# High and low words of the split weights interleaved in one SBUF tile, on a two-block forward pass

## What is computed

```
first_block:  h = x + y @ w_out          y = [conv group, pool group] of rmsnorm(x) @ w_in + b_in
              h = h + swiglu(rmsnorm(h)) w_gate, w_up: 1024 x 2816, w_down: 2816 x 1024
              return rmsnorm(h)
second_block, layer 0:  gated ("fox") attention, 16 heads of 64; layer norm; conv FFN; layer norm; shared k1, k2, v
              layer 1:  differential attention, 8 heads; layer norm; conv FFN; layer norm
conv FFN:     u = x @ w_in (1024 x 5632); causal conv of width 3 over tokens; silu(g) * val; @ w_out (2816 x 1024)
```

## Time and profile before

| | us |
|---|---|
| three runs, median | 1811.86 |
| three runs, lowest and highest | 1810.9, 1812.83 |
| the profiled execution, its own time | 1808.84 |
| span from its first to its last instruction | 1807.0 |
| TensorE busy | 1762.7 |
| weight loads busy, beside the matmuls | 1476.5 |
| VectorE, ScalarE, GpSimd busy | 765.9, 796.0, 1032.3 |

### The profile page before, as it was taken

How to read it: one execution, slowest core, us unless ns; L and a number is a source line. 1 busy time by engine, 2 the same in 40 slices (tenths; PEclk the granted TensorE clock), 3 DMA queues, 4 the chain that set the end, 5 groups by cost and what they waited for, 6 DMA issues and landing times.

```text
span 1807.0 us, 26859 instructions
## 1 busy us (share of the span) xinstructions
PE 1762.7 (98%) x8755; PEld 1476.5 (82%) x8755; DVE 765.9 (42%) x1382; ACT 796.0 (44%) x1674; POOL 1032.3 (57%) x926
## 2 busy tenths in 40 slices
PE   8999999999999999999999999999999999999997
PEld 6879888888887888788888888877777888888887
DVE  7973000001235556553333322487875533333224
ACT  5644332322245555464444422555565644444231
POOL 6966555555562333466666665655554666666651
PEclk9999999999999999999999999999999999999999
DMA  4312333333334454223333233333332233332332
GB/s 153 94 47 82 105 93 93 93 88 109 94 89 115 126 134 120 85 75 100 103 94 93 82 110 88 82 93 78 86 82 71 72 110 97 93 101 82 105 91 98
DMA packets 327252, 171.94 MB, mean 95 GB/s; under 512 B 43458, under 2 KB 316948, under 8 KB 327188
## 3 DMA queue, kind: packets, MB, share of 16 engines
q1 hardware_dynamic: 327172, 171.12, 33.7%
q10 hardware_dynamic: 16, 0.00, 0.0%
HBM read 152.15 MB, written 2.10 MB: 85 GB/s over the span
## 4 chain that ended last, share of the span: by engine, by line
PE 86%; DVE 9%; ACT 2%; issue 1%; POOL 1%; DMA 0%; DVEq 0%; SPq 0%; ACTq 0%
PE bank L983 24%; PE bank L985 23%; PE bank L984 23%; DVE score L2266 3%; PE attended L983 2%; PE attended L984 2%; PE attended L985 2%; PE turned L1424 1%; PE attended L1440 1%; PE bank L1056 1%; PE bank L1068 1%; DVE xres L2165 1%; PE bank L1069 0%; PE score L1417 0%; PE score L1407 0%
## 5 line engine op out<-in xcount | busy, mean ns | idle before, releaser
L742 POOL TENSOR_TENSOR WL<-raw,WH 128x512 fp32r<-128x512 f32 (+3 forms) x656 | 777.6, 1207 | 539.8 <-ACT WH L1605 537.2
L983 PE MATMUL bank<-XL,WH 128*128 128x512 f32 x1432 | 568.5, 397 | 3.7 <-DVE work L2577 1.2
L985 PE MATMUL bank<-XH,WL 128*128 128x512 f32 x1432 | 557.9, 390 | 0.0
L984 PE MATMUL bank<-XH,WH 128*128 128x512 f32 x1432 | 557.3, 389 | 0.0
L1605 ACT ACTIVATE WH<-raw 128x512 fp32r<-128x512 f32 (+3 forms) x656 | 338.4, 566 | 293.2 <-PE bank L985 186.5
L985 PEld LDWEIGHTS bank<-XH,WL 128*128 128x128 f32 x1432 | 269.4, 188 | 56.9
L983 PEld LDWEIGHTS bank<-XL,WH 128*128 128x128 f32 x1432 | 269.7, 188 | 55.9 <-DVE work L2577 1.5
L984 PEld LDWEIGHTS bank<-XH,WH 128*128 128x128 f32 x1432 | 269.9, 188 | 50.3
L983 PE MATMUL bank<-HL,WH 128*128 128x512 f32 (+1 forms) x528 | 198.6, 376 | 0.0
L985 PE MATMUL bank<-HH,WL 128*128 128x512 f32 (+1 forms) x528 | 198.4, 376 | 0.0
L984 PE MATMUL bank<-HH,WH 128*128 128x512 f32 (+1 forms) x528 | 198.4, 376 | 0.0
(11 more groups left out here) (366 smaller groups left out, 2524.9 us busy)
## 6 DMA issues: line engine op xcount, KB each, us to landing
raw<-in_ffn_w_in SPq DMA_DIRECT2D x88, 512.0 KB, 3.7
raw<-in_w_gate SPq DMA_DIRECT2D x22, 512.0 KB, 3.6
raw<-in_w_up SPq DMA_DIRECT2D x22, 512.0 KB, 3.7
raw<-in_ffn_w_out SPq DMA_DIRECT2D x28, 384.0 KB, 3.2
raw<-in_ffn_w_out SPq DMA_DIRECT2D x28, 320.0 KB, 3.2
raw<-in_a_w_in SPq DMA_DIRECT2D x16, 512.0 KB, 3.9
raw<-in_kv_w SPq DMA_DIRECT2D x32, 256.0 KB, 3.0
raw<-in_w_in SPq DMA_DIRECT2D x12, 512.0 KB, 3.7
```

The costliest lines, as they stand in the source:

```text
L742: pool.tensor_tensor(wl, x, wh, ALU.subtract).then_inc(w_lo, 1)
L983: pe.matmul(out_, wh, xl, start=start, stop=False)
L984: pe.matmul(out_, wh, xh, start=False, stop=False)
L985: return pe.matmul(out_, wl, xh, start=False, stop=stop)
```

## The change

WH and WL were two tiles, each of 4 slots of 8 x 128 words in a partition. They become views of one tile with a last dimension of 2: high words at even, low words at odd places. All code that uses WH and WL stays as it is, so each access to them, by ScalarE (write), GpSimd (read and write) and TensorE (weight load), now has a step of two words, 8 bytes, where it had one of 4. The space in a partition is the same, 32 KB.

```
-        WH = sb("WH", [P, SLOTS, DT, P], F32R)
-        WL = sb("WL", [P, SLOTS, DT, P], F32R)
+        weights = sb("weights", [P, SLOTS, DT, P, 2], F32R)
+        WH, WL = weights[:, :, :, :, 0], weights[:, :, :, :, 1]
```

## The result

The changed kernel takes 1852.34 us (median of four runs, 1851.71 to 1857.44) against 1811.38 us for the kernel before in the same comparison: ratio 1.0233, 95% interval 1.0219 to 1.0247. It is slower by 41 us. The forecast was 1811.9 us, with a range to 1819 us. The profiled execution has a span of 1851.0 us, 44.0 us longer than before.

The account below looks back on a forecast made before the run. TensorE was taken as the bound, busy 1762.7 of 1807.0 us. Zero each for TensorE, ScalarE and GpSimd, added to the median of 1811.86 us, gave 1811.9 us, with a range from 1808.5 to 1819 us.

Parts of the forecast that it names:

- What bounds the kernel: Whole kernel: TensorE is the bound, busy 1762.7 of 1807.0 us, and hardly ever waits for weights, 1.3 us.
- ScalarE and GpSimd at zero: Stepped write of WH, read of WH and write of WL: claimed to add 0 us each to the kernel.
- high ends: Upper bounds for the stepped accesses of ScalarE and GpSimd: twice the time of now, 1242 ns for ScalarE's write.
- I take zero: TensorE's stepped weight loads: claimed to cost nothing, from L2242's 6 ns in 256 words and the moving stream's pace.
- It could take twice as long and just stay hidden: Under 512-column matmuls a weight load has 0.226 us and needs 0.113, so twice its time was claimed to cost nothing.
- the range's upper end: 1819 us: the small producer slowdown, and 0.006 us more on each 256-column matmul, 7 us.
- The last sign that I gave: In the changed profile: 512-column starts moving from 0.226 us would mean a weight load of over twice its time.
- the forecast's own rule: 512-column matmuls: they keep 0.226 us until loads need more than that, and pay beyond it.
- The 0.006 us margin at 256 columns: Under 256-column matmuls a load has 0.119 us and needs 0.113, so nearly all of any slowdown is paid.
- the rival's price: 256-column matmuls with loads at half pace: from 0.119 to 0.226 us, 1164 x 0.107 = 125 us.
- The rival that came true in sign, a slower weight load: Weight loads slow down and TensorE pays in 256-column stretches: 1871 us at 0.170 us, 1937 at 0.226; chance 14%.
- The rule I set beside it: Full rate needs adjacent word pairs, else some 1.7 times the time: loads at 0.19 us, about 85 us more.

Follow-up runs that it names:

- f3_writers_step: Against the kernel before: one tile, ScalarE and GpSimd access every other word, TensorE reads blocks of 128 neighbouring words; 1811.34 us, ratio 1.0005.
- step-4 runs: Kernel before with TensorE reading weights at every fourth word: 2001.78 us, ratio 1.1065; and m1_streams rows at step 4: 17.09 us at 512 columns.
- f7_step_256: Against the kernel before: TensorE reads every other word in the 256-column matmuls only, writers at unit step; 1812.5 us, ratio 1.0008.
- m1_streams: Separate kernel, rows of 72 matmuls with weight words 1 to 16 apart; at 512 columns a row takes 16.49 us at unit step, 16.96 at step 2.
- f2_pe_step: Against the kernel before: one tile, only TensorE reads every other word, ScalarE and GpSimd write blocks at unit step; 1855.14 us, ratio 1.0243.

## Why the prediction was wrong

**What bounds the kernel** was right: TensorE's pace is the kernel's time, and the producers of weights are hardly ever waited for (1.3 us before, 1.4 us after). The chain, and its counterpart, says so on both sides.

**ScalarE and GpSimd at zero** was right for the time. Their stepped accesses cost 41 and 17 ns of 621 and 1363, far below the high ends, and f3_writers_step shows that the kernel doesn't feel them.

**"I take zero" for the weight load** was the first error, of a small size. It rested on L2242, a row of another engine, on 64 partitions. Its 6 ns in 256 words were dismissed as nothing. TensorE's load loses 7 ns in 128 words.

**"It could take twice as long and just stay hidden"** was the step that failed. I compared the pace of loads alone, 0.113 us, with the pace of 512-column matmuls, 0.226 us, and called the difference a margin. At a step of two the loads alone need 0.118 us, so nearly all of that margin was left. Yet the 512-column starts went from 0.226 to 0.2331 and 0.2355 us. Load and matmul overlap, but their pace isn't simply that of the longer one. With 6108 such matmuls, each ns is 6.1 us; the range's upper end allowed 7 us for 1164 short matmuls and nothing for these. The last sign that I gave failed with it: I wrote that moved 512-column starts would mean a load of over twice its time, and they moved with a load that went from 188 to 196 ns.

There was a hint in the rows, though no proof. By the earlier trace rows a column takes (0.226 - 0.119) / 256 = 0.42 ns, so 512 columns need 0.214 us, and 12 ns of the 0.226 us aren't columns. That says that a pair of load and matmul costs something that the columns don't explain, and I should have left a term open for it. It doesn't say where the step shows: the 256-column matmuls have the same 12 ns and pay nothing.

The step-4 runs don't test this step. Their loads need 0.232 us, more than the 0.226 us, so by the forecast's own rule the 512-column matmuls go to 0.232 us; they go to 0.235.

**The 0.006 us margin at 256 columns** was read the wrong way too. I expected nearly all of any slowdown to be paid there. The stepped loads need 0.118 us and stay below the 0.120 us of these matmuls, and f7_step_256 finds no cost. For a load twice as long the rival's price was sound: 0.232 us in m1_streams where I had 0.226.

The rival that came true in sign, a slower weight load, had 14%, and its place was the wrong one. The rule I set beside it gave too much: "Vector Engine (DVE) Microarchitecture Reference", section "Measured stream behaviour on trn2" of the Trainium skill, by which I worked out 0.19 us a load; the load came to 0.118. The 16-byte line in "SBUF — State Buffer" of the Trainium skill, section "Door 1: The DMA port swizzle", fits better: by it two words used of each line are enough for full speed, and the load at step 2 is indeed only 6% slower; at step 4, one word a line, it takes 0.232 against 0.111 us. The same passage calls a stride of 4 fp32 free, and that the runs contradict. The 7 ns that a 512-column matmul loses at step 2 are in neither.

## What to carry to other kernels

Keep the words of a stationary operand next to each other where full-length matmuls bound the time; here a step of two words cost 2.3%, a step of four 10.7% (most of it in the 256-column ones), and writers with the step cost nothing. Don't take time to spare for a proof that a longer load is hidden: here loads needed 0.118 of 0.226 us and each 512-column matmul still paid 7 to 9 ns. Multiply one such small term by the count of matmuls, and leave that much room in the range. A microbenchmark of one row per length and step takes one run and would have settled this.

## What the runs showed of the hardware that I had not expected

- The next matmul's start moves in jumps: rows of 504 to 512 columns at unit step all have about 0.2267 us, and with every load at step 2 it is 0.2267 us from 500 to 508 columns and 0.2333 us from 510. With one load of three at step 2 it is 0.231 us at 508 columns already.
- With loads at step 2 TensorE can settle in paces of 0.2331 and 0.2355 us in different loops (gu1 against down0) and keep them over the stage; gu1 itself has the one pace in the changed kernel and the other in f2_pe_step.
- The weight load's time against the step, by median in m1_streams at 512 columns: 188 ns at 1, 193 at 2, 253 at 3, 310 at 4, 329 at 8.
- One stepped load in three costs more than half of what all three cost, in the whole kernel (23.6 of 45.3 us) and in the row alone (4.2 of 6.5 ns).
